# Expert stage of a two-layer encoder trunk: gate and up projections with the weight strips stationary and 88 token columns moving, one copy of the unit in TensorE's loop, and the down banks cleared by ScalarE

## The reference, cut to what matters

```python
def moe_swiglu(h, w_router, b_router, w_gu, w_down):
    logits = (h @ w_router).astype(jnp.float32) + b_router.astype(jnp.float32)
    top_logit, top_idx = lax.top_k(logits, TOP_K)          # TOP_K = 2 of N_EXPERTS = 8
    top_w = jax.nn.softmax(top_logit, axis=-1)
    gates = jnp.sum(jax.nn.one_hot(top_idx, N_EXPERTS) * top_w[..., None], axis=-2)
    out = jnp.zeros_like(h)
    for e in range(N_EXPERTS):
        out = out + gates[..., e:e + 1] * swiglu(h, w_gu[e], w_down[e])
    return out
```

## Time and profile before

| | |
|---|---|
| median of 3 runs | 1382.06 us (1381.54 to 1383.05) |
| time of the profiled execution | 1381.95 us |
| its span | 1380.2 us |
| TensorE busy | 1370.3 us (99%) |
| weight loads busy | 1180.8 us |
| VectorE busy | 675.7 us |
| ScalarE busy | 311.2 us |
| granted TensorE clock | 1.00, which is 2.4 GHz |
| transfers | 448.60 MB, mean 325 GB/s |

### The profile page before, as it was taken

The page is one execution under the profiler, slowest core; times in us unless marked ns, Lnnn a source line. Parts: engine busy times, 40 slices in busy tenths (PEclk is TensorE's granted clock), DMA queues, the critical chain, the costliest instruction groups (busy, mean ns, idle before and its releaser), DMA issues.

```text
span 1380.2 us, 43324 instructions
## 1 busy us (share of the span) xinstructions
PE 1370.3 (99%) x18179; PEld 1180.8 (86%) x18179; DVE 675.7 (49%) x1677; ACT 311.2 (23%) x514; POOL 40.8 (3%) x61
## 2 busy tenths in 40 slices
PE   8999999999999999999999999999999999999998
PEld 6888888888788888898888888888888888889996
DVE  7886555556886533522433432532433342244544
ACT  7565444446533200100000000000010010011112
POOL 1010000000000000000000000000000000000000
PEclk9999999999999999999999999999999999999999
DMA  9477555546424999999999999999999999999970
GB/s 318 178 246 247 190 189 193 185 168 244 154 94 160 382 394 409 409 400 409 408 403 408 408 401 409 406 398 409 408 397 410 407 408 397 409 397 409 410 298 31
DMA packets 123591, 448.60 MB, mean 325 GB/s; under 512 B 14476, under 2 KB 14476, under 8 KB 122896
## 3 DMA queue, kind: packets, MB, share of 16 engines
q1 hardware_dynamic: 119232, 435.21, 82.1%
q0 software_dynamic: 4160, 12.58, 2.7%
q10 hardware_dynamic: 144, 0.03, 0.0%
HBM read 442.71 MB, written 7.34 MB: 326 GB/s over the span
## 4 chain that ended last, share of the span: by engine, by line
PE 99%; DVE 1%; issue 0%; ACT 0%; POOL 0%; POOLq 0%; DVEq 0%; ACTq 0%
PE PS L970 43%; PE PS L541 10%; PE PS L543 10%; PE PS L542 10%; PE PS L1005 9%; PE PS L1014 9%; PE PS L968 2%; PE PS L592 1%; PE PS L1009 1%; PE PS L836 0%; PE PS L682 0%; PE PS L610 0%; PE PS L1104 0%; PE PS L946 0%; PE PS L926 0%; PE PS L884 0%
## 5 line engine op out<-in xcount | busy, mean ns | idle before, releaser
L2050 DVE STREAM_TRANSPOSE he<-junk 32x96 f32<-32x96 f32 x880 | 237.5, 270 | 212.2 <-PE PS L1005 180.4
L970 PE MATMUL PS<-raw,gain 128*32 128x384 f32 x2712 | 328.1, 491 | 0.0
L970 PE MATMUL PS<-SC,gain 128*32 128x384 f32 x2664 | 323.3, 491 | 0.0
L968 PE MATMUL PS<-raw,gain 128*32 128x128 f32 x2712 | 305.6, 273 | 0.0
L968 PE MATMUL PS<-SC,gain 128*32 128x128 f32 x2664 | 299.8, 273 | 0.0
L968 PEld LDWEIGHTS PS<-SC,gain 128*32 128x32 f32 x2664 | 290.9, 110 | 8.2
L968 PEld LDWEIGHTS PS<-raw,gain 128*32 128x32 f32 x2712 | 295.3, 110 | 0.2
L541 PE MATMUL PS<-w_hi,xT_hi 128*128 128x512 f32 x536 | 213.0, 397 | 0.9 <-DVE w_lo L1533 0.9
L543 PE MATMUL PS<-w_lo,xT_hi 128*128 128x512 f32 x536 | 209.0, 390 | 0.0
L542 PE MATMUL PS<-w_hi,xT_lo 128*128 128x512 f32 x536 | 208.7, 389 | 0.0
L1426 ACT ACTIVATE junk<-PS 128x384 f32<-128x384 f32 x56 | 27.7, 495 | 763.2 <-PE PS L970 763.2
(11 more groups left out here) (312 smaller groups left out, 1514.9 us busy)
## 6 DMA issues: line engine op xcount, KB each, us to landing
raw<-in_e_w_gu SPq DMA_DIRECT2D x226, 512.0 KB, 8.3
SC<-in_e_w_gu SPq DMA_DIRECT2D x222, 512.0 KB, 8.3
SC<-in_e_w_down SPq DMA_DIRECT2D x114, 512.0 KB, 8.3
raw<-in_e_w_down SPq DMA_DIRECT2D x110, 512.0 KB, 8.3
raw<-in_ffn_w_gu SPq DMA_DIRECT2D x44, 512.0 KB, 4.9
raw<-in_w_in_c SPq DMA_DIRECT2D x32, 512.0 KB, 5.1
raw<-in_ffn_w_down SPq DMA_DIRECT2D x22, 512.0 KB, 5.2
raw<-in_w_in_ab SPq DMA_DIRECT2D x20, 512.0 KB, 6.7
```

What stands on the lines that cost most here:

```text
L968: pe.matmul(PS[CAP:P, bank, k * P:(k + 1) * P], tokens[k], w[:, MAIN:N], start=start and k == 0, stop=stop, skip_group_check=True)
L970: m = pe.matmul(PS[32 * k:32 * (k + 1), bank, 0:MAIN], tokens[k], w[:, 0:MAIN], start=start, stop=stop, skip_group_check=True)
L2050: m = dve.transpose(block[to:to + 32, :].rearrange("p (b c) -> p b c", c=P)[:, :, of:of + 32], hh[of:of + 32, 0:MAIN].rearrange("p (b c) - ...
```

## The change

- `CAP` falls from 96 to 88 tokens; the slots stay 96 wide (`SLOTS`).
- **Gate and up** (`feature_strips` in place of `strips`): 32 columns of the weight matrix are stationary and the 88 token columns move. A k-tile of one side has 16 matmuls of 88 columns, four in each column group, in place of six of 128 and 384 columns. The result has hidden features on partitions and tokens along the bank.
- **VectorE** no longer transposes the hidden block: `unit_turn` is one copy of 128 x 384.
- **ScalarE** clears banks 4 and 5 after it has taken out an item's output (semaphore `y_clear`), and all down rounds accumulate (`start=False`).
- **TensorE's loop** has one copy of the unit: an outer loop over all items, with `turn_rows` ahead of the first unit, and an inner loop over the units. TensorE waits for `table_ready` ahead of the outer loop, and VectorE makes the tables before it waits for the first unit.
- **`last_down`** uses the wide form with bank 4 first for all four rounds, then bank 5; the routing transpose (`turn_sel`) moves behind the loop.
- The transfers, their sizes and their order stay.

```diff
-    CAP = 96
-    MAIN = 4 * CAP
+    CAP = 88
+    SLOTS = 96
+    MAIN = 4 * SLOTS
...
-            def strips(bank, tokens, w, start, stop):
-
-                for k in range(CAP // 32):
-                    pe.matmul(PS[CAP:P, bank, k * P:(k + 1) * P], tokens[k], w[:, MAIN:N], start=start and k == 0, stop=stop,
-                              skip_group_check=True)
-                    m = pe.matmul(PS[32 * k:32 * (k + 1), bank, 0:MAIN], tokens[k], w[:, 0:MAIN], start=start, stop=stop,
-                                  skip_group_check=True)
-                return m
-
+            def feature_strips(side, k, w):
+
+                for b in range(4):
+                    for f in range(4):
+                        m = pe.matmul(PS[32 * f:32 * (f + 1), side, b * SLOTS:b * SLOTS + CAP], w[:, b * P + 32 * f:b * P + 32 * (f + 1)],
+                                      xe[:, k, :], start=(k == 0 and b == 0), stop=(k == KT - 1), skip_group_check=True)
+                return m
...
-                    pe.wait_ge(h_ready, i * EU + (FB + 1))
-                    unit_gu(G_MOE + 4, i * EU, (0,))
...
-                    pe.wait_ge(sel_ready, i + 3)
-                    turn_rows()
...
-                unit_gu(G_MOE + 4, i * EU, (1,))
-                pe.wait_ge(y_evac, i + 1)
...
+            def last_down(g, n, turns):
+
                 pe.wait_ge(hT_ready, n)
...
+                rounds = [(turned_tokens(2 * j + r, he_last), raw_part(g + j, r)) for j in range(2) for r in range(2)]
+                for n, both in enumerate(rounds):
+                    landed(g + n // 2, n % 2, turns)
+                    bank4(0, *both)
+                    rest(0, *both)
+                    bank4(1, *both)
+                    rest(1, *both)
+                    m = bank4(2, *both)
+                m.then_inc(y_half, 1)
+                for both in rounds:
+                    bank5(0, *both)
+                    rest(2, *both)
+                    bank5(1, *both)
+                    bank5(2, *both).then_inc(used, 1)
+
+            def unit(i, n):
+                pe.wait_ge(go_act, n + 1)
+                pe.wait_ge(go_dve, n + 1)
+                pe.wait_ge(h_ready, n + (FB + 1))
+                unit_gu(G_MOE + 4, n)
+                pe.wait_ge(y_clear, i + 1)
+                unit_down(G_MOE + 8, n + (FB + 1), n)
...
-            item(0, False, True)
             pe.wait_ge(table_ready, 1)
             last_item = pe.value_load(itab[0:1, 0:1], min_val=E - 1, max_val=ITEMS - 1)
-            with pe.Fori(1, last_item) as i:
-                item(i, False)
-            item(last_item, True)
+            with pe.Fori(0, last_item + 1) as i:
+                pe.wait_ge(sel_ready, i + 3)
+                turn_rows()
+                with pe.Fori(0, EU - (i >= last_item)) as u:
+                    unit(i, i * EU + u)
+            turn_sel()
...
                 m.then_inc(y_evac, 1)
+                act.wait_ge(y_evac, i + 1)
+                for c in range(2):
+                    m = act.activation(PS[:, 4 + c, :], zeros[:, :], ACT.Copy)
+                m.then_inc(y_clear, 1)
...
-                for to in range(0, P, 32):
-                    for of in range(0, P, 32):
-                        m = dve.transpose(block[to:to + 32, :].rearrange("p (b c) -> p b c", c=P)[:, :, of:of + 32],
-                                          hh[of:of + 32, 0:MAIN].rearrange("p (b c) -> p b c", c=P)[:, :, to:to + 32])
-                m.then_inc(hT_ready, 1)
+                dve.tensor_copy(block[:, :], hh[:, 0:MAIN]).then_inc(hT_ready, 1)
...
+            step(dve.memset(hid_cols[:, :, CAP:SLOTS], 0.0))
+            tables()
             dve.wait_ge(used, 2 * (G_MOE + 4))
             unit_hidden(FB + 1)
+            dve.sem_inc(go_dve, 1)
             next_rows(0)
             unit_turn(FB + 1)
-            tables()
```

More of the change, by code:

```diff
@@ L194, in trunk @@
         xe = gain[:, 0:KT * CAP].rearrange("p (k c) -> p k c", c=CAP)
-        xg_turned = xn[:, 0, 0:KT * CAP].rearrange("p (k c) -> p k c", c=CAP)
+        hid_cols = hh[:, 0:MAIN].rearrange("p (b c) -> p b c", c=SLOTS)
+        gate_out, up_out = (PS[:, side, 0:MAIN].rearrange("p (b c) -> p b c", c=SLOTS)[:, :, 0:CAP] for side in range(2))
+        xg_turned = xn[:, 0, 0:KT * SLOTS].rearrange("p (k c) -> p k c", c=SLOTS)
         ye = raw[:, 0, 0:D]
@@ L986, in unit_gu @@
                             landed(granule, j // 2, turns)
-                        m = strips(side, [xe[:, k, c:c + 32] for c in range(0, CAP, 32)],
-                                   raw_part(granule, j // 2)[:, j % 2 * N:(j % 2 + 1) * N], k == 0, k == KT - 1)
+                        m = feature_strips(side, k, raw_part(granule, j // 2)[:, j % 2 * N:(j % 2 + 1) * N])
                         if j % 2:
@@ L1027, in unit_down, with bank4, bank5 @@
-            def unit_down(g, n, turns, first=False):
+                return [block[:, b * SLOTS + a:b * SLOTS + a + 32] for a in range(0, SLOTS, 32)]
+            def bank4(k, tokens, w):
+                return pe.matmul(PS[32 * k:32 * (k + 1), 4, :], tokens[k], w[:, 0:N], start=False, stop=True,
+                                 skip_group_check=True)
+            def bank5(k, tokens, w):
+                return pe.matmul(PS[32 * k:32 * (k + 1), 5, 0:N // 2], tokens[k], w[:, N:N + N // 2], start=False,
+                                 stop=True, skip_group_check=True)
@@ new lines, in rest, with wide_round @@
+            def rest(k, tokens, w):
+                c = k % 2 * (N // 2)
+                return pe.matmul(PS[SLOTS:P, 4 + k // 2, c:c + N // 2], tokens[k], w[:, N + N // 2:2 * N], start=False,
+                                 stop=True, skip_group_check=True)
+            def wide_round(g, j, r):
+                both = turned_tokens(2 * j + r), raw_part(g + j, r)
+                rest(0, *both)
[3 more added lines that the diff above has]
+                bank4(1, *both)
+                bank5(2, *both)
+                rest(2, *both)
+                bank5(0, *both)
+                return bank4(2, *both)
@@ L1031, in unit_down @@
                         landed(g + j, r, turns)
-                        m = wide_round(g, j, r, first and j == 0 and r == 0)
-                        m.then_inc(used, 1)
-            def unit_down_last(g, n, turns, first=False):
-                pe.wait_ge(hT_ready, n)
-                for j in range(2):
-                    for r in range(2):
-                        landed(g + j, r, turns)
-                        for c in range(2):
-                            m = down_round(g, j, r, c, first and j == 0 and r == 0, True)
-                        m.then_inc(used, 1)
+                        wide_round(g, j, r).then_inc(used, 1)
@@ L1486, in _ @@
             ended = last_item * EU + EU
-            for c in range(2):
-                if c == 0:
-                    act.wait_ge(y_half, Y_MOE + 1)
-                else:
-                    product(G_MOE, ended)
-                act.activation(ye[0:CAP, c * N:c * N + MAIN], PS[0:CAP, 4 + c, 0:MAIN], ACT.Copy).then_inc(ye_act, 1)
+            act.wait_ge(tsel_psum, 1)
+            act.activation(selT[0:CAP, :, :], PS[0:CAP, 2, 0:T * P].rearrange("p (t c) -> p t c", t=T),
+                           ACT.Copy).then_inc(selT_ready, 1)
+            act.wait_ge(y_half, Y_MOE + 1)
+            act.activation(ye[0:SLOTS, 0:N], PS[0:SLOTS, 4, :], ACT.Copy).then_inc(ye_act, 1)
+            product(G_MOE, ended)
+            act.activation(ye[0:SLOTS, N:N + N // 2], PS[0:SLOTS, 5, 0:N // 2], ACT.Copy).then_inc(ye_act, 1)
             def square_acc(t):
@@ L2022, in turn_xg @@
                 for to in range(0, P, 32):
-                    for of in range(0, CAP, 32):
+                    for of in range(0, SLOTS, 32):
                         m = dve.transpose(xg_turned[to:to + 32, :, of:of + 32],
@@ L2190, in _ @@
                 item(i, False)
+            dve.sem_inc(sel_ready, 1)
             last_turn(last_item)
```

116 lines of the change are left out of this document (36 added, 80 removed).

## The result

The changed kernel took **1396.16 us** (1394.83 to 1396.23, three runs) against 1382.06 us before: a ratio of 1.0095, 95% interval 1.0075 to 1.0115. It is 14 us slower; the prediction said 4.4 us faster, and its range ended at 1395. The profiled execution after has a span of 1394.4 us, 14.2 more than before. One execution of the kernel before, timed beside the second group of experiments, took 1765 us at a granted clock of 0.75; it is left out of every comparison.

The account below looks back on a forecast made before the run. The prediction saw two close limits, TensorE at 15.66 us per unit and transfers at 15.36 plus indirect transfers. End 2.6, expert part 2.5, takeout 0.5, less start 1.2, gave 4.4 us off: 1377.7 us, range 1371 to 1395.

Parts of the forecast that it names:

- What bounds the kernel: Expert part: two close limits, TensorE at 15.66 us per unit and transfers at 15.36 plus the indirect transfers.
- Gate and up on TensorE: Gate and up: passes of 88 columns take 77 ns, so TensorE's unit is 15.06 us, 0.60 less.
- At nothing: Items counted as costing or gaining nothing: ScalarE's clears, saved transposes, routing ahead of later items, the loop's code staying on chip.
- the rival on code: TensorE's loop: its code is fetched again at each turn, about +360 us; chance 0.05.
- What of the 0.60 us remains: Expert part: transfers cap TensorE's gain per unit; 0 to 6.9 us can be won back, 2.5 taken.
- The end: After the last half lands at 1338.9 us, the last down ends at 1341.5 in place of 1344.13: 2.6 us won.
- the takeout: VectorE's takeout of the second half at the end is shorter, so the second scatter waits some 0.5 us less.
- The start: Before the second unit: TensorE awaits VectorE's routing behind the tables moved ahead; 1.2 us lost, between 0 and 3.
- The wait for VectorE: Before the second unit, TensorE waits 1.4 us for VectorE's routing up to `sel_ready`.
- The sum again: Whole kernel: 2.6 + 2.5 + 0.5 - 1.2 = 4.4 us less, giving 1377.7 us.

Follow-up runs that it names:

- the edit of the transfers: Gate and up from the second unit on in megabyte transfers instead of half-megabytes: on the changed kernel 1381.54 us, on the kernel before 1382.49 us.
- the run with 64 columns: Changed kernel with 64 weight columns stationary in two groups in place of 32 in four, throughout gate and up: 1382.28 us, ratio 0.9997.
- the kernel with the old gate and up: Changed kernel with the earlier gate and up (tokens stationary, 96 rows) and VectorE's 32 x 32 transposes back: 1385.30 us, ratio 1.0024.
- thinning both: Changed kernel, indirect gather of x and scatter of y moving 2 rows in place of 88 from the second item on: 1377.13 us.
- the one in 4 KB pieces: 64 columns and megabyte transfers throughout, each megabyte read and laid down as 4 KB pieces that don't touch: 1384.81 us, ratio 1.0019.

## Why the prediction was wrong, by its steps

**What bounds the kernel: right.** TensorE at 15.66 us, transfers at 15.36: the units after are 15.36 us to the hundredth, half-megabytes land after 13.4 us, and the edit of the transfers moves the one kernel and not the other.

**Gate and up on TensorE: right.** From the chain of the kernel after:

```profile
533.03 9.71 PE PS L977 x509
```

128 passes in a group take 9.71 us, 76 ns each for the 77 predicted; a unit 14.87 for 15.06. The rule of the Trainium skill (TensorE: Matmul & The Clock Gate, section on the gap of 56 ns), 25 ns between starts however small the matmul, does not hold here: four groups together start a pass every 19 ns (76/4); the page doesn't say what forms of matmul its number covers, so the prediction's reason for the difference is not shown.

**At nothing: this is the step that failed.** "The loop has about 1,200 TensorE records [...] so such a loop stays on the chip." It does stay (no such transfer from 520 to 1330 us), and the rival on code asked only whether it is fetched again. The working put at nothing, without a reason, what it costs to come **for the first time**. The change made the first unit's gate and up, written out ahead of the loop, 2.7 times as many instructions (16 matmuls per k-tile and side for 6), and each is so short that 256 of them, one piece of code, are used up in some 2.6 us. The rows for this stood in the prediction: 6 matmuls of 0.655 us became 16 of 0.61 (eight passes of 76 ns in each group), so the same time needs 2.7 times the code. No row of before showed how fast code comes, and that should have been an unknown with an upper end, not nothing. Measured: 12.4 us of "issue" and some 1.7 of clock, 14.3 us at the third SiLU against the run with 64 columns. The Trainium skill, Runtime: NRT & Kernel Launch, section Instruction fetch mechanics, calls the cost of crossing a 16 KB boundary mostly hidden. Here it was not: nine pieces cost 12.4 us of waits, seven 3.8, five 0.6.

**What of the 0.60 us remains: 2.5 predicted, nothing measured.** From the third SiLU to the last the changed kernel takes 0.6 us less than before, and the kernel with the old gate and up takes 0.6 less too. TensorE did win 6.0 us by the 16th SiLU (4.8 with 64 columns, where no such loss at the start had to be made good), but with that the queue's slack was spent. Then the mean item became 0.3 us longer (110.2 against 109.95), since a queue without slack shows what the indirect transfers cost (thinning both took 17.8 us off), and the read back in the last item, for which the working had no term, took 6.5 and gave back 2.5.

**The end: 2.6 predicted, 0.1 measured.** It rested on TensorE waiting for the last half-megabyte. But the 2 MB read back in the last item held TensorE up once (the step of 22.2 us), and behind 1285 us the profile has no wait of TensorE. From the last SiLU to the first scatter are 13.64 us, before 13.76. Behind it 0.3 us were won, where the takeout was to give 0.5.

**The start: 1.2 predicted, 4.0 measured** at the second SiLU for all of the change but gate and up, 2.8 in the kernel's time. The wait for VectorE was 1.4 us, as read; what was missing is the clock, granted at 0.86 and 0.79 behind the idle time. That is not the same in every execution: of two runs above with one program for TensorE, wide strips and megabyte transfers, one had 1.00 from 470 to 480 us (third SiLU at 497.76) and the one in 4 KB pieces 0.90 and 0.76 (499.54).

**The sum again** with what was measured: start +15.3, repaid 6.0, items +1.4, the read back +6.5 and -2.5, the end -0.4. With the code's 14 us mended the kernel comes to 1382, no change, as the run with 64 columns shows: a gain of 4.4 us would not have come either.

## What to carry to other kernels

Count the instructions of straight-line code per microsecond wherever a change makes them shorter: a loop's first turn counts as straight-line code, and waits named "issue" in a chain, with transfers of instructions beside them, are its mark. When two limits are 2% apart, as here, taking one away can buy less than the difference, since it also spends the slack that hid other costs. So change both together: strips of 64 columns and 8 KB pieces gave nothing against before each by itself, and 13 us together, 18 with down's too. And compare two forms of a loop by the stretch behind its first turn before choosing by the total time: the 11.3 us between narrow and wide strips lay ahead of that stretch.

## What the runs showed of the hardware

- Code came in pieces of 16 KB, nine of them in some 36 us while TensorE waited for it (4.6 us from one to the next); 128 passes and their loads, a piece, were executed in 2.6 us, and TensorE went on 2 to 3 us behind a piece's packets. A loop of some 1,200 TensorE instructions was not fetched again in 800 us.
- With pieces of 4 KB the 16 engines stood at 409.6 GB/s (6.29 MB in 15.36 us) whether a transfer had half a megabyte or one; with pieces of 8 KB they reached 422 where all transfers had them and 418 where two thirds did.
- Transfers of 64 partitions of 8 KB each, in turn for the lower and the upper half, ran at 248 GB/s (500 to 585 us) and 342 (620 to 1230 us) with all engines busy, and the time varied between 1575 and 1936 us.
- With 64 stationary float32 columns in each of two groups a pass of 88 columns took 78.5 ns, with 32 in each of four 76; a step of 2 in the stationary operand cost nothing (units of 15.190 against 15.187 us).
